# Where the head of each feed-forward layer puts its products, and which engine adds its weight blocks

## The chip, the cores and the metric

The kernel runs on one core of a Trainium2 chip. The metric is the device time in microseconds of one execution; of three executions of the kernel before, the median was 2402.97 us (2402.32 to 2407.87). The profile comes from one further execution, whose own time was 2399.43 us. Its records span 2397.6 us, and all times in rows are counted from the start of that span.

## The reference

One inference step of a streaming encoder with two layers, for 512 prompt tokens and 32 sample tokens, which the kernel handles together as 544 token columns. Each layer is a feed-forward block, a mixer (attention with a gated recurrence, or a gated delta rule) and a second feed-forward block. The change touches the four feed-forward blocks alone:

```python
def swiglu(h, w_in, w_out):
    gate, up = jnp.split(h @ w_in, 2, axis=-1)
    return (jax.nn.silu(gate) * up) @ w_out

x = x + 0.5 * swiglu(rms_norm(x, ffn1_norm[layer]), ffn1_w_in[layer], ffn1_w_out[layer])
```

The width of the model is 1024, the hidden width 2816. Everything is float32, and the result has to be nearly as exact as float32.

## The kernel before

**Three products for one.** Each float32 weight block and each activation is split into a high part (rounded, written by ScalarE, `op_split_hi`, L767) and a low part (the difference, written by VectorE, `op_split_lo`, L773). TensorE multiplies high by high, high by low and low by high and adds the three in PSUM.

**Units.** The hidden width is cut into 11 pairs of units of 256 columns. Unit `s = 0` of a pair is the gate, unit `s = 1` the value that the gate multiplies. Of one feed-forward layer the units are, in TensorE's order: unit 0 (kind "whole") and units 1, 2, 3 (kind "plain", 4 blocks of 24 matmuls each), which are the head. They give the first two pairs. Then come nine pairs in which each unit is of the kind "seven": the 2x2 block product of a unit is done with seven block products in place of eight (a Strassen-like scheme), at 12 matmuls each. It needs four sums and differences of weight blocks per unit, `wsum`, and seven token operands, `bop`, which are made once per layer in the head: sums in `bopf` (`token_sum`, L1054), then high parts (`bop_split_hi`, L926) and low parts (`bop_split_lo`, L932). After each of the pairs 2 to 9 a "mid" unit (4 blocks of 24 matmuls) multiplies part of the hidden activations by `w_out` and adds it to `x` (`x_update`, L1192). Four "last" units end the layer. So unit 4 is the gate and unit 5 the value of the first pair of the kind seven, and unit 6 is the first mid unit.

**What sets the order.** Nothing is scheduled by a planner: each engine runs a list of instructions written out by hand and waits on semaphores in that order. An instruction that waits holds back all that stands behind it on its engine. The splits of unit u+1 are made while TensorE works on unit u, in a ring of 8 blocks (`entry`), of which each is free again when TensorE has used it. Raw weights come in by a queue of SyncE into two buffers, `raw[0]` and `raw[1]`; a buffer is loaded again when all blocks of its unit are split.

**Copies that TensorE waits for.** In a seven unit ScalarE copies four PSUM banks to SBUF (`m1c`, `m5c`, `u2c`, `u3c`, L1134). TensorE's third block waits for the first copy, its fourth for the second, its fifth for the third, its seventh for the fourth (`ffn_seven_pe`). VectorE then adds the pieces (L1211, L1214, L1221).

**The hidden products of the head.** For pair j of the head VectorE multiplies the gate by the value out of PSUM (`hidden`, L1048), ScalarE makes the high part (`hidden_hi`, L911) and VectorE the low part (`hidden_lo`, L916). In the kernel before, those of the second pair close the head's lists on both engines. The sums of weights of units 4 and 5 are made by GpSimd (`weight_sums`, L1000 to L1005), those of the other 16 seven units of a layer by VectorE (`weight_sum_dve`, L1016 to L1024).

## Time and profile before

| What | Value |
|---|---|
| Median of 3 executions | 2402.97 us |
| The profiled execution's own time | 2399.43 us |
| Its span | 2397.6 us |
| TensorE busy | 2321.1 us, 97% |
| VectorE busy | 1656.8 us, 69% |
| ScalarE busy | 1061.9 us, 44% |
| GpSimd busy | 352.4 us, 15% |
| Mean granted TensorE clock | 0.990 |

TensorE is busy in nearly the whole span, so a stretch in which it has nothing to do is what there is to be looked for. In the rows PE is TensorE, DVE is VectorE, ACT is ScalarE, POOL is GpSimd. A line of the view in order of time gives start and duration in us, engine, line of the kernel, operation, what is written and read, the shapes and how many instructions are merged in it; in square brackets stands how long the engine sat idle before it, and what ended that.

### The profile page before, as it was taken

What the parts mean: (1) busy time and instruction counts of PE and PEld (TensorE: products, weight loads), DVE (VectorE), ACT (ScalarE), POOL (GpSimd) and SP (SyncE); (2) the same over time, 40 slices, a digit from 0 to 9 for tenths busy, and PEclk for the clock granted to TensorE, in tenths of its full rate; (3) what the DMA queues carried; (4) which work ended last, traced back from release to release, by engine and by line L of the source; (5) the groups of instructions that cost most, each with busy time, mean ns of one, the idle gap of its engine ahead of it and who ended that gap; (6) DMA issues with size and microseconds to landing.
All of it is one profiled execution on the core that took longest, in us unless ns stands there. A gap on an engine that the chain in (4) does not pass through costs nothing.

```text
span 2397.6 us, 44509 instructions
## 1 busy us (share of the span) xinstructions
PE 2321.1 (97%) x18296; PEld 2263.3 (94%) x18296; DVE 1656.8 (69%) x2657; ACT 1061.9 (44%) x1951; POOL 352.4 (15%) x284
## 2 busy tenths in 40 slices
PE   7899999999999899999899999999999999899998
PEld 7899999988989899999899999999999899899998
DVE  6867776656575877776866776788655657776674
ACT  3544444333323444444444444455345543444443
POOL 2300001000042300001400000243033533200001
PEclk9999999999999999999999999999999999999999
DMA  3223223322202232222232232322200012223222
GB/s 111 88 89 106 89 99 106 97 89 85 69 10 88 71 106 89 99 96 89 71 105 89 90 105 89 100 71 89 77 25 2 10 43 90 71 89 106 89 85 77
DMA packets 174905, 194.70 MB, mean 81 GB/s; under 512 B 4810, under 2 KB 155726, under 8 KB 174697
## 3 DMA queue, kind: packets, MB, share of 16 engines
q1 hardware_dynamic: 161902, 181.64, 23.0%
q10 hardware_dynamic: 12162, 8.11, 1.2%
q8 instruction: 147, 2.41, 0.4%
q0 software_dynamic: 640, 2.10, 0.3%
q14 instruction: 54, 0.44, 0.1%
HBM read 185.73 MB, written 6.10 MB: 80 GB/s over the span
## 4 chain that ended last, share of the span: by engine, by line
PE 88%; DVE 7%; issue 2%; ACT 1%; POOL 0%; DMA 0%; ACTq 0%; DVEq 0%
PE ps L852 32%; PE ps L782 25%; PE ps L659 19%; PE ps L3067 1%; DVE wl L773 1%; PE ps L3052 1%; DVE bop L932 1%; PE ps L3198 1%; DVE bopf L938 1%; DVE wl L644 1%; PE ps L3040 1%; PE ps L1637 0%; DVE bopf L1054 0%; PE ps L2105 0%; PE ps L2202 0%
## 5 line engine op out<-in xcount | busy, mean ns | idle before, releaser
L852 PE MATMUL ps<-bop,wh 128*128 128x272 f32 x4032 | 771.6, 291 | 36.2 <-ACT m1c L1134 33.0
L852 PEld LDWEIGHTS ps<-bop,wh 128*128 128x128 f32 x4032 | 639.5, 190 | 37.6 <-issue 33.8
L852 PE MATMUL ps<-bop,wl 128*128 128x272 f32 x2016 | 586.7, 291 | 0.0
L773 DVE TENSOR_TENSOR wl<-raw,wh 128x512 fp32r<-128x512 f32 (+1 forms) x456 | 318.0, 708 | 295.9 <-ACT wh L767 290.7
L852 PEld LDWEIGHTS ps<-bop,wl 128*128 128x128 f32 x2016 | 382.5, 190 | 0.0
L767 ACT ACTIVATE wh<-raw 128x512 fp32r<-128x512 f32 (+1 forms) x456 | 263.8, 609 | 222.4 <-PE ps L782 185.1
L782 PE MATMUL ps<-hh,wh 128*128 128x288 f32 (+1 forms) x1408 | 290.2, 287 | 0.0
L782 PE MATMUL ps<-hl,wh 128*128 128x288 f32 (+1 forms) x1408 | 289.6, 287 | 0.0
L782 PE MATMUL ps<-hh,wl 128*128 128x288 f32 (+1 forms) x1408 | 288.6, 286 | 0.0
L659 PE MATMUL ps<-xh,wh 128*128 128x288 f32 x1088 | 233.0, 295 | 3.4 <-DVE wl L644 2.8
L659 PE MATMUL ps<-xl,wh 128*128 128x288 f32 x1088 | 224.8, 288 | 0.0
L659 PE MATMUL ps<-xh,wl 128*128 128x288 f32 x1088 | 224.0, 287 | 0.0
L782 PEld LDWEIGHTS ps<-hh,wh 128*128 128x128 f32 x1408 | 215.0, 188 | 6.0 <-issue 6.0
L782 PEld LDWEIGHTS ps<-hh,wl 128*128 128x128 f32 x1408 | 215.2, 188 | 0.0
L782 PEld LDWEIGHTS ps<-hl,wh 128*128 128x128 f32 x1408 | 214.7, 188 | 0.0
L767 ACT ACTIVATE wh<-wsum 128x512 fp32r<-128x512 f32 x256 | 159.6, 627 | 109.4 <-DVE wsum L1016 83.4
L692 POOL COPY ssq<-sq 128x544 f32<-128x544 f32 x7 | 5.2, 743 | 1296.4 <-ACT sq L678 1296.4
L773 DVE TENSOR_TENSOR wl<-wsum,wh 128x512 fp32r<-128x512 f32 x256 | 175.2, 684 | 17.6 <-ACT wh L767 13.9
L659 PEld LDWEIGHTS ps<-xh,wh 128*128 128x128 f32 x1088 | 166.9, 189 | 15.4 <-issue 7.4
L659 PEld LDWEIGHTS ps<-xh,wl 128*128 128x128 f32 x1088 | 167.0, 189 | 0.0
L659 PEld LDWEIGHTS ps<-xl,wh 128*128 128x128 f32 x1088 | 166.7, 189 | 0.0
L644 DVE TENSOR_TENSOR wl<-raw,wh 128x2048 fp32r<-128x2048 f32 x41 | 94.5, 2305 | 39.7 <-ACT wh L639 39.7
(475 smaller groups left out, 3750.2 us busy)
## 6 DMA issues: line engine op xcount, KB each, us to landing
raw<-ffn_w_in SPq DMA_DIRECT2D x88, 1024.0 KB, 5.1
raw<-ffn_w_out SPq DMA_DIRECT2D x32, 1024.0 KB, 5.0
raw<-odd_w_in SPq DMA_DIRECT2D x16, 1024.0 KB, 5.7
raw<-even_w_in SPq DMA_DIRECT2D x14, 1024.0 KB, 5.1
raw<-ffn_w_out SPq DMA_DIRECT2D x16, 768.0 KB, 4.2
raw<-even_w_out SPq DMA_DIRECT2D x4, 1024.0 KB, 4.9
raw<-odd_w_out SPq DMA_DIRECT2D x4, 1024.0 KB, 5.2
xnat<-x_prompt SPq DMA_DIRECT2D x2, 1024.0 KB, 12.0
```

Source lines behind the costliest of these rows:

```text
L644: nc.vector.tensor_tensor(wl[slot][:, 0:kt, :], raw[slot][:, 0:kt, :], wh[slot][:, 0:kt, :].bitcast(F32), ALU.subtract).then_inc(lo_done.s ...
L659: ins = nc.tensor.matmul(ps[:, 2 * pe_out + b, PCOLS[b]], w, r[:, rk, TOKENS[b]], start=first and a == 0, stop=last and a == 2)
L767: nc.scalar.activation(entry(op)[0][:, 0:block_nk(u, i), :], op_source(u, i), ACT.Copy).then_inc(op_hi.sem, 1)
L773: nc.vector.tensor_tensor(lo[:, 0:nk, :], op_source(u, i), hi[:, 0:nk, :].bitcast(F32), ALU.subtract).then_inc(op_lo.sem, 1)
L782: ins = nc.tensor.matmul(ps[:, 2 * pe_out + b, PCOLS[b]], w[:, k, :], r[:, rk + k, TOKENS[b]], start=first and k == 0 and a == 0, stop=las ...
L852: ins = nc.tensor.matmul(ps[:, bank, 0:TH], w[:, k, :], bop[:, r, k, :], start=i in S_OPEN and k == 0 and a == 0, stop=k == KH - 1 and a = ...
L932: nc.vector.tensor_tensor(bop[:, o, :, :], bopf[:, o, :, :], bop[:, 7 + o, :, :].bitcast(F32), ALU.subtract).then_inc(bop_lo.sem, 1)
L938: nc.vector.scalar_tensor_tensor(out=bopf[:, first:first + 2, k % KH, :], in0=two(x[:, k, :]), scalar=gain(n, k), in1=two(rstd[:]), op0=AL ...
L3040: ins = nc.tensor.transpose(bank(g, 2, n, n)[:, h, :], dX[g][0:n, h, 0:n], ident[0:n, 0:n])
L3052: ins = nc.tensor.matmul(bank(g, 0, n, n)[:, h, :], strict[0:n, h, 0:n], dX[g][0:n, h, 0:n], start=True, stop=True)
L3067: ins = nc.tensor.matmul(bank(g, 0, n, n)[:, h, :], dU[g][0:n, h, 0:n], dZ[g][0:n, h, 0:n], start=True, stop=True)
L3198: ins = nc.tensor.matmul(ps[:, 2 * (2 * q + c) + b, PCOLS[b]], w, r[:, k, TOKENS[b]], start=k == 0 and a == 0, stop=k == KT - 1 and a == 2)
```

## The change

Two things are written in another way.

**The head's order.** The product of the second pair of the head, its high part and its low part leave the head's lists. The product (now `lead_product`) is issued by VectorE in unit 4, behind the fourth split of unit 5; its low parts and ScalarE's high parts are issued in unit 5. The low parts of the first pair go to unit 4. On ScalarE and VectorE the rest of the head is put in the order in which TensorE uses it: the token operands come earlier, and the weight sums of unit 4 are made by VectorE between them. The small `lam_dve` goes to the end of the head in the first layer.

**Who adds weight blocks.** Of a layer's 18 seven units GpSimd summed 2 (units 4 and 5) and VectorE 16. Now GpSimd sums the gate's unit of pairs 3 to 10, which is 8 units, and VectorE the other 10. GpSimd makes them as soon as the raw weights are there and the sums of the unit before are made. VectorE's list of each mid unit loses four sums by this.

```diff
@@ ffn_lead_act (ScalarE, head)
+        bop_split_hi(act, f, 0)
+        for i in range(4):
+            op_split_hi(act, units[3], i)
+        bop_split_hi(act, f, 1)
+        bop_split_hi(act, f, 2)
         hidden_hi(act, units[1], 0, 1)
         hidden_hi(act, units[1], 1, 2)
...
-        hidden_hi(act, units[3], 0, 1)
-        hidden_hi(act, units[3], 1, 2)
+        op_split_hi(act, units[4], 5)
+        op_split_hi(act, units[4], 6)
@@ ffn_lead_pool (GpSimd, head)
         gate(0, 0)
         gate(0, 1)
-        weight_sums(pool, ffns[f][4])
         gate(1, 0)
         gate(1, 1)
@@ weight_sum_dve
-        if s - first_seven[u.f] < 2:
+        if u.s == 0 and s != first_seven[u.f]:
             return
@@
+    def lead_product(dve, u, c):
+        dve.wait_ge(gate_rstd.sem, gate_rstd.at(2 * LEAD_PAIRS * u.f + 2 * u.pair + c + 1))
+        dve.wait_ge(op_used.sem, op_used.at(u.op + 2 * c + 2))
+        if u.pair:
+            dve.wait_ge(hl_ready.sem, hl_ready.at(2 * FJ * u.f + c + 1))
+        nc.vector.tensor_tensor(two(sq[c][:]), halves(2 + c), two(gbuf[c][:]), ALU.mult).then_inc(h_made.sem, 1)
+
+    def weight_sums_pool(pool, u):
+        s, slot, out = u.seven, u.raw % 2, sums_of(u)
+        pool.wait_ge(raw_loaded[slot].sem, raw_loaded[slot].at(8 * (u.raw - slot) + 16))
+        pool.wait_ge(sum_made.sem, sum_made.at(4 * s))
+        pool.wait_ge(op_lo.sem, op_lo.at(sevens[s - 2].op + 5))
...
     def ffn_pool(pool, f, n):
         ffn_lead_pool(pool, f, n)
         for u in ffns[f]:
-            if u.kind == "seven" and u.at > 2 * LEAD_PAIRS:
-                if u.seven - first_seven[f] < 2:
-                    weight_sums(pool, u)
+            if u.kind == "seven" and u.s == 0 and u.seven != first_seven[f]:
+                weight_sums_pool(pool, u)
@@ ffn_lead_dve (VectorE, head), gate of the second pair
                 dve.wait_ge(op_used.sem, op_used.at(units[2 * j].op + 2 * c + 2))
+                dve.wait_ge(h_made.sem, h_made.at(2 * FJ * f + c + 1))
...
-        hidden(1, 0)
...
-        hidden(1, 1)
-        hidden_lo(dve, units[3], 0, 1)
-        hidden_lo(dve, units[3], 1, 2)
@@ ffn_seven_act, behind the fourth split
         late_act(act, ffns[u.f][u.at - 1])
+        if u.at == 2 * LEAD_PAIRS + 1:
+            hidden_hi(act, ffns[u.f][u.at - 2], 0, 1)
+            hidden_hi(act, ffns[u.f][u.at - 2], 1, 2)
@@ ffn_seven_dve, behind the fourth split
+        if u.at == 2 * LEAD_PAIRS:
+            for c in range(2):
+                hidden_lo(dve, ffns[u.f][1], c, c + 1)
+            for c in range(2):
+                lead_product(dve, before, c)
+            dve.wait_ge(h_made.sem, h_made.at(2 * FJ * u.f + 2 * LEAD_PAIRS))
+        if u.at == 2 * LEAD_PAIRS + 1:
+            for c in range(2):
+                hidden_lo(dve, ffns[u.f][u.at - 2], c, c + 1)
+            dve.wait_ge(hl_ready.sem, hl_ready.at(2 * FJ * u.f + 2 * LEAD_PAIRS))
```

**VectorE from the end of the head into unit 4, first layer.** `wl` from `wsum_first_70` are splits of unit 4, from `wsum_first_71` of unit 5; L1048 is the product, L916 its low part. Before:

```order
L932 TENSOR_TENSOR bop<-bopf,bop 128x1088
L1048 TENSOR_TENSOR sq<-ps,gbuf_68 128x544
L773 TENSOR_TENSOR wl<-wsum_first_70,wh 128x512
L932 TENSOR_TENSOR bop<-bopf,bop 128x1088
L773 TENSOR_TENSOR wl<-wsum_first_70,wh 128x512
L773 TENSOR_TENSOR wl_50<-wsum_first_70,wh_49 128x512
L773 TENSOR_TENSOR wl_50<-raw,wh_49 128x512 x2
L1048 TENSOR_TENSOR sq<-ps,gbuf_69 128x544
L916 TENSOR_TENSOR hl<-sq,hh 128x544 x2
L773 TENSOR_TENSOR wl_50<-raw,wh_49 128x512
L773 TENSOR_TENSOR wl<-wsum_first_71,wh 128x512 x3
L1211 TENSOR_TENSOR gbuf_68<-u2c_78,ps 128x272
```

And now, from the first weight sum of unit 5 on (the product is L1016, the addition L1226):

```order
L1000 TENSOR_TENSOR wsum_first_71<-raw 128x512
L773 TENSOR_TENSOR wl_50<-raw,wh_49 128x512
L1003 TENSOR_TENSOR wsum_first_71<-wsum_first_71,raw 128x512
L773 TENSOR_TENSOR wl<-wsum_first_71,wh 128x512
L1006 TENSOR_TENSOR wsum_first_71<-raw,wsum_first_71 128x512
L773 TENSOR_TENSOR wl<-wsum_first_71,wh 128x512
L1008 TENSOR_TENSOR wsum_first_71<-raw 128x512
L773 TENSOR_TENSOR wl<-wsum_first_71,wh 128x512
L916 TENSOR_TENSOR hl<-sq,hh 128x544 x2
L1016 TENSOR_TENSOR sq<-ps,gbuf_68 128x544
L1016 TENSOR_TENSOR sq<-ps,gbuf_69 128x544
L1226 TENSOR_TENSOR gbuf_68<-u2c_78,ps 128x272
```

The products of the second pair stood among unit 4's splits and ahead of all of unit 5's; they now stand behind four splits of unit 5.

**ScalarE at the same place.** L911 is the high part of the hidden product, L1134 (now L1136) a copy that TensorE waits for. Before:

```order
L767 ACTIVATE wh_49<-wsum_first_70 128x512
L767 ACTIVATE wh_49<-raw 128x512 x2
L911 ACTIVATE hh<-sq 128x544 x2
L767 ACTIVATE wh_49<-raw 128x512
L1134 ACTIVATE m1c_74<-ps 128x272
L767 ACTIVATE wh<-wsum_first_71 128x512
```

And now:

```order
L767 ACTIVATE wh_49<-wsum_first_70 128x512
L926 ACTIVATE bop<-bopf 128x1088
L767 ACTIVATE wh_49<-raw 128x512 x3
L1136 ACTIVATE m1c_74<-ps 128x272
L767 ACTIVATE wh<-wsum_first_71 128x512
L1136 ACTIVATE m5c_76<-ps 128x272
```

The two high parts that stood ahead of the copy `m1c` are gone from here.

**VectorE at the start of a mid unit.** L1182 is the last product of the pair, `wsum_72` the sums of the next gate's unit, L1192 the first update of `x`. Before:

```order
L1182 TENSOR_TENSOR sq<-ps,gbuf_69 128x272
L1016 TENSOR_TENSOR wsum_72<-raw 128x512
L773 TENSOR_TENSOR wl<-raw,wh 128x512
L1019 TENSOR_TENSOR wsum_72<-wsum_72,raw 128x512
L773 TENSOR_TENSOR wl<-wsum_72,wh 128x512
L1022 TENSOR_TENSOR wsum_72<-raw,wsum_72 128x512
L1024 TENSOR_TENSOR wsum_72<-raw 128x512
L916 TENSOR_TENSOR hl<-sq,hh 128x544
L1192 SCALAR_TENSOR_TENSOR x<-ps,x 128x544
```

And now:

```order
L1187 TENSOR_TENSOR sq<-ps,gbuf_69 128x272
L773 TENSOR_TENSOR wl<-raw,wh 128x512
L773 TENSOR_TENSOR wl<-wsum_72,wh 128x512
L916 TENSOR_TENSOR hl<-sq,hh 128x544
L1197 SCALAR_TENSOR_TENSOR x<-ps,x 128x544
```

Four instructions between the last product and the first update have left VectorE's list; they are GpSimd's now.

## Rows read from the trace of the kernel before

**Rows 1.** The page, part 1: busy time, share of the span, instructions.

```profile
PE 2321.1 (97%) x18296; PEld 2263.3 (94%) x18296; DVE 1656.8 (69%) x2657; ACT 1061.9 (44%) x1951; POOL 352.4 (15%) x284
```

**Rows 2.** Waits of PE: us in total, times, longest us.

```profile
PE ps L852 <- ACT m1c L1134: 33.0, 4, 8.9
PE ps L852 <- DVE wl L773: 3.2, 3, 1.4
```

**Rows 3.** Timeline of PE: starts of units 4, 5 and 6, four layers.

```profile
80.96 0.41 PE L852 MATMUL ps<-bop,wh 128*128 128x272 f32 x2
...
92.75 0.79 PE L852 MATMUL ps<-bop,wh 128*128 128x272 f32 x2 [8.04 <-ACT m1c L1134]
...
101.63 0.42 PE L852 MATMUL ps<-bop,wh 128*128 128x272 f32 x2
...
112.23 0.42 PE L782 MATMUL ps<-hh,wh 128*128 128x288 f32 x2
...
804.97 0.41 PE L852 MATMUL ps<-bop,wh 128*128 128x272 f32 x2
...
827.61 0.42 PE L852 MATMUL ps<-bop,wh 128*128 128x272 f32 x2
...
1189.13 0.41 PE L852 MATMUL ps<-bop,wh 128*128 128x272 f32 x2
...
1210.51 0.42 PE L852 MATMUL ps<-bop,wh 128*128 128x272 f32 x2
...
2046.40 0.41 PE L852 MATMUL ps<-bop,wh 128*128 128x272 f32 x2
...
2069.48 0.42 PE L852 MATMUL ps<-bop,wh 128*128 128x272 f32 x2
```

**Rows 4.** Timeline of ACT, end of the first layer's head.

```profile
91.14 0.66 ACT L911 ACTIVATE hh<-sq 128x544 fp32r<-128x544 f32 x1 [4.63 <-DVE sq L1048]
91.71 0.61 ACT L767 ACTIVATE wh<-raw 128x512 fp32r<-128x512 f32 x1
92.23 0.38 ACT L1134 ACTIVATE m1c<-ps 128x272 f32<-128x272 f32 x1
```

**Rows 5.** Timeline of DVE, same place.

```profile
78.80 2.38 DVE L932 TENSOR_TENSOR bop<-bopf,bop 128x1088 fp32r<-128x1088 f32 x1
...
85.12 0.71 DVE L1048 TENSOR_TENSOR sq<-ps,gbuf 128x544 f32<-128x544 f32 x1
...
86.79 1.28 DVE L932 TENSOR_TENSOR bop<-bopf,bop 128x1088 fp32r<-128x1088 f32 x1
88.00 1.28 DVE L773 TENSOR_TENSOR wl<-wsum_first,wh 128x512 fp32r<-128x512 f32 x2
...
90.40 0.71 DVE L1048 TENSOR_TENSOR sq<-ps,gbuf 128x544 f32<-128x544 f32 x1
```

**Rows 6.** Timeline of POOL, same place: first and last sum of unit 5.

```profile
78.29 1.75 POOL L1000 TENSOR_TENSOR wsum_first<-raw 128x512 f32<-128x512 f32 x1
...
84.01 2.31 POOL L1005 TENSOR_TENSOR wsum_first<-raw 128x512 f32<-128x512 f32 x1
```

**Rows 7.** Timeline of DVE, second layer's head: products of the first pair.

```profile
785.14 1.34 DVE L1048 TENSOR_TENSOR sq<-ps,gbuf 128x544 f32<-128x544 f32 x2
```

**Rows 8.** The page, part 6: DMA issues, KB each, us to landing.

```profile
raw<-ffn_w_in SPq DMA_DIRECT2D x88, 1024.0 KB, 5.1
```

**Rows 9.** Timeline of DVE, second half of unit 5 and start of unit 6.

```profile
107.33 0.69 DVE L773 TENSOR_TENSOR wl<-raw,wh 128x512 fp32r<-128x512 f32 x1 [5.65 <-ACT wh L767]
...
109.00 0.69 DVE L773 TENSOR_TENSOR wl<-raw,wh 128x512 fp32r<-128x512 f32 x1 [0.60 <-ACT wh L767]
...
112.90 0.43 DVE L1182 TENSOR_TENSOR sq<-ps,gbuf 128x272 f32<-128x272 f32 x1
...
117.50 0.71 DVE L1192 SCALAR_TENSOR_TENSOR x<-ps,x 128x544 f32<-128x544 f32 x1
```

**Rows 10.** Timeline of PE, unit 6: its third block.

```profile
118.36 0.49 PE L782 MATMUL ps<-hh,wh 128*128 128x288 f32 x2
```

More of the change, by code:

```diff
@@ L1065, in ffn_lead_dve @@
             bop_normed(dve, f, n, k)
+        token_sum(3, 7, 6, 4, 0)
         op_split_lo(dve, units[2], 0)
-        token_sum(3, 7, 6, 4, 0)
         op_split_lo(dve, units[2], 1)
@@ L1071, in ffn_lead_dve @@
         op_split_lo(dve, units[2], 2)
+        op_split_lo(dve, units[2], 3)
+        token_sum(2, 5, 3, 8, 1)
         token_sum(1, 5, 7, 8, 0)
[L1073 to L1079 removed]
+        token_sum(0, 4, 2, 8, 2)
+        lead_product(dve, units[1], 0)
+        lead_product(dve, units[1], 1)
+        bop_split_lo(dve, f, 0)
         for i in range(4):
             op_split_lo(dve, units[3], i)
+        gate(1, 0)
+        weight_sum_dve(dve, units[4], 0)
+        bop_split_lo(dve, f, 1)
+        weight_sum_dve(dve, units[4], 1)
+        bop_split_lo(dve, f, 2)
+        op_split_lo(dve, units[4], 0)
+        weight_sum_dve(dve, units[4], 2)
+        gate(1, 1)
+        op_split_lo(dve, units[4], 1)
+        bop_split_lo(dve, f, 3)
+        weight_sum_dve(dve, units[4], 3)
+        op_split_lo(dve, units[4], 2)
+        bop_split_lo(dve, f, 4)
+        op_split_lo(dve, units[4], 3)
+        bop_split_lo(dve, f, 5)
+        op_split_lo(dve, units[4], 4)
+        bop_split_lo(dve, f, 6)
+        op_split_lo(dve, units[4], 5)
+        op_split_lo(dve, units[4], 6)
         if f == 0:
             lam_dve(dve)
[L1084 to L1099 removed]
     def next_split(eng, split, u, place):
```

61 lines of the change are left out of this document (13 added, 48 removed).

## The prediction

> **What bounds the kernel now.** I read the page's busy times first. TensorE is busy in 97% of the span [rows 1], so a gain has to come from the remaining idle time or from slow matmuls. The view of who waited for whom, cut to TensorE, shows the idle time: 33.0 us in four waits of up to 8.9 us for ScalarE's copy `m1c`, and 3.2 us for VectorE's splits `wl` [rows 2]. Four is the number of feed-forward layers. The timeline of TensorE shows the place: unit 4, the first of the kind seven [rows 3]. A unit of seven blocks normally takes 112.23 - 101.63 = 10.60 us, so a block takes 1.51. From the start of unit 4 to that of unit 5 it is 20.67, 22.64, 21.38 and 23.08 us in the four layers [rows 3], 87.8 together, where 42.4 would do. So the heads lose 45.4 us. 36.2 of these are the waits; the other 9.2 are matmuls after them that run slower (a pair takes 0.79 us right behind the wait, 0.41 otherwise [rows 3]), 2.3 us per head.
>
> Why the copy comes late stands in the timelines of ScalarE and VectorE. ScalarE could copy at 82.5, when the first block is done, but its list has a high part of the hidden product ahead; it sits 4.63 us for that and copies only at 92.23 [rows 4]. What it waits for is VectorE's product at 90.40, which stands behind all splits of unit 4 [rows 5]. And these are late because low parts of the token operands take 2.38 us while GpSimd sums weights, and 1.28 when it doesn't [rows 5, 6].
>
> **Part 1: the head.** The product and its high and low parts leave the place ahead of the copy, so that wait goes. What is late next is VectorE's own list. I lay it out in the second layer, where the head is shortest. VectorE finishes the products of the first pair at 786.5 [rows 7]. The list from there to the end of the head is seven low parts of operands at 1.21 (86.79 to 88.00), eleven splits and four sums at 0.60 each (two splits take 1.28 with the last one's tail), two gate products at 0.64 (a product's 0.71 less the tail that the next one covers) [rows 5]: 8.5 + 9.0 + 1.3 = 18.8. GpSimd's eight sums of the head are gone; its two gate multiplications of the second pair stay and hold VectorE up by 2.38 - 1.28 = 1.1 each. So the head's list ends at 786.5 + 18.8 + 2.2 = 807.5. Unit 4 starts at 804.97 [rows 3] and needs its last block's operands at 804.97 + 6 x 1.51 = 814.0, so no block of unit 4 waits for a split.
>
> Inside unit 4, two things are due. First, the copy `m5c` must be done before the fourth block, at 809.5; ScalarE's list has ahead of it a split of unit 5's first sum. That sum is done at 807.5 + 0.6, the split 0.6 later, the copy 0.4 later: 809.1, with 0.4 to spare. Second, the hidden products of the second pair must be there when unit 5 starts, at 815.6: three more sums and four splits (7 x 0.6) and two low parts and two products (4 x 0.64) end at 814.9, 0.7 to spare. Both margins are thin, but no wait is left by this count. Cost of part 1: -45.4 us. A bound on the other side: every us that VectorE is later beyond the 0.4 becomes a wait of TensorE, once per layer.
>
> **Part 2: the sums on GpSimd.** They are off TensorE's path if VectorE isn't pushed. One deadline is already missed a little: the third block of a mid unit needs VectorE's first update of `x`, which in unit 6 runs from 117.50 to 118.21 [rows 9]; TensorE starts the block at 118.36 [rows 10], about 0.18 later than it could. So whatever moves this update moves TensorE, in all 32 mid units.
>
> What GpSimd costs I take from the head. Its sum takes 1.75 us from 78.29 but had to wait for VectorE until 78.80, so it needs 1.24 alone. VectorE's instruction of 78.80 then waits for GpSimd's end at 80.04 and is done 1.14 later. They take turns. A VectorE instruction that has an input in PSUM isn't touched: 0.71 us inside GpSimd's last sum, and 0.71 without [rows 5, 6].
>
> Now a steady pair, in the clock of rows 9. The raw weights of the next gate are requested when unit 5's last split is done, near 101.7, and land 5.1 us later [rows 8], at 106.8. VectorE is idle until 107.33 [rows 9]. GpSimd's four sums then end at 108.15, 109.9, 111.6 and 113.1, and VectorE's instructions with two inputs in SBUF between them at 108.6 (first split), 110.3 (second), 111.8 (an addition), 113.5 (third split). Left before the last product are a product 0.35, an addition 0.35, a split 0.60 and a product 0.64, so it starts at 115.5 where it now starts at 112.90 [rows 9]: 2.6 later. From there to the update it is 4.60 now, of which the four sums moved away are 2.40; so the update starts at 115.47 + 2.20 = 117.67, 0.17 later than now. Waits of 0.60 and less that VectorE has in this stretch pay for part of it. The bounds for a mid unit: if the sums fell wholly into VectorE's idle time the 0.18 would be won back; if each of the four costs its full 1.1 and nothing is absorbed, it is 4.4 - 2.4 = 2.0 us lost. I take 0.17, the value of the layout. For the 28 mid units with a steady pair before them: +4.8 us.
>
> The first mid unit of each layer is worse. VectorE enters unit 4 late by 2.5 and has 4 sums, 7 splits, 2 low parts, 2 products and 3 additions in it, 10.3 us, and is done at 817.8, 2.2 after unit 5's start instead of at it. The raw weights land later by as much, at 109.0 in the clock of rows 9, when VectorE is no longer idle; and unit 5 has the two moved low parts besides. From 109.0 the list to the last product is 5.1 us alone, the four turns cost 4.4 less some 0.2 of waits, and 2.2 follow: the update starts at 120.5 and ends at 121.1, 2.9 later than now. Three layers at 2.9 and the first at 2.2, since there the head's list ends 1.7 behind unit 4's start: +11 us. Bounds: 0 (all absorbed), and 5 per layer.
>
> The two high parts that ScalarE now has in unit 5 take 1.2 us and push its fourth copy to about 110.5; the seventh block is due at 101.63 + 9.08 = 110.71, so I cost it at nothing.
>
> In the Trainium skill, page SBUF — State Buffer, section Who interferes with whom, the port that VectorE's second input and GpSimd share is an exclusive lock that an instruction keeps to its end. That is the mechanism of rival (e); the rows of the head agree with it in kind, but show 1.10 us lost and not GpSimd's whole instruction, and I go by the rows.
>
> **Sum.** -45.4 + 4.8 + 11 = -29.6 us. Against the profiled execution's own 2399.4 this is 2369.8. The median shown is 3.5 us above that execution; for the median I forecast 2402.97 - 29.6 = 2373 us.
>
> **Rivals.**
> (a) The mid units come free. GpSimd's sums meet VectorE's idle time and its PSUM instructions more than I laid out, the update is early everywhere: -45.4 - 32 x 0.18 = -51, or 2352. For it speaks the 5.65 us that VectorE idles before 107.33 [rows 9]; against it, that the weights land only at 106.8.
> (b) A wait stays in the heads. If VectorE comes into unit 4 one us later than I count, the fourth block or unit 5's first waits. That is about 1 us, and if the clock falls again 2.3 more: 4 x 3.4 = +14, or 2387. For it speak the thin margins.
> (c) Slower: the shared port is dear in every pair. The update of `x` is pushed by 2.0 us in 28 mid units and by 5 in four: -45.4 + 56 + 20 = +31, or 2434. It decides where a mid unit loses more than 45.4 / 32 = 1.4 us on average, that is where the pair's last product starts later than 116.7 in the clock of rows 9. For it speaks that GpSimd's sums took about 2.3 us each in places [rows 6]; against it, that VectorE's waits and its PSUM instructions lie between.
> (d) The change only trades waits: ScalarE is late for the copies by splits of unit 5 that wait for sums now on VectorE, and TensorE gets the same 8 us at another block. About 2400. Against it: the layout has these sums 0.4 us ahead of their need.
> (e) Each turn costs VectorE the whole 1.24 us that GpSimd needs, in place of the 1.10 of rows 5: four turns of 0.14 in 32 mid units are +18, or 2391. Against it: no instruction in rows 5 pays that much.
>
> **Chances.** The forecast 0.53, with a range of its own of 2363 to 2384 (0 to 1 us per head, first mid units between 0 and 5). (a) 0.15, (b) 0.17, (c) 0.06, (d) 0.05, (e) 0.04. A measurement of this kernel tells about 0.3%, 7.2 us, from no change. The forecast, (a), (b) and (e) are faster by more than that, and a fifth of (d): 0.90. Half of (d), and those of (c) in which the loss just balances, are the same: 0.04. Slower: 0.06. For 8 in 10 I leave out (c), (d) and the lower half of (a): 2351 to 2394.
>
> **What would show it.** Head right: no wait of TensorE for `m1c` in unit 4, 10.6 to 11 us from unit 4's start to unit 5's in all four layers, no slow pairs there, GpSimd without sums in the head. Head wrong: a wait of about 1 us at the fourth block or at unit 5's first. Port right: GpSimd's sums start about 5.2 us after unit 5's start at 1.3 to 1.8 us each, VectorE's splits there take up to 1.8, the last product starts 2.6 later against TensorE than now, and the third block of a mid unit is late by some 0.35 us; the first mid unit of a layer by about 3. What would make the whole wrong is a mid unit that loses more than 1.4 us, or a head that still waits.

## The result, and the profile after the change

| | Before | After |
|---|---|---|
| Median | 2402.64 us (2400.74 to 2407.87, 4 executions) | 2372.49 us (2370.07 to 2375.44, 4 executions) |
| Profiled execution, its own time | 2399.43 us | 2370.07 us |
| Its span | 2397.6 us | 2368.3 us |
| Mean granted TensorE clock | 0.990 | 0.997 |

The changed kernel is faster by 1.3%: 0.9872 of the time before, with a 95% interval of 0.985 to 0.9893. The forecast was 2373 us, and 2369.8 for the profiled execution.

The page's busy times after the change, which answer to [rows 1]:

```profile
PE 2311.4 (98%) x18296; PEld 2254.8 (95%) x18296; DVE 1677.0 (71%) x2561; ACT 1056.7 (45%) x1951; POOL 491.7 (21%) x380
```

VectorE has 96 instructions fewer than before and is busy 20.2 us longer. Its splits of raw weights take 867 ns on average where they took 708, and GpSimd's sums pay too (the four groups take 1.31, 1.63, 1.63 and 1.52 us for one sum, where the forecast counted 1.24 for one alone). From the page's costliest groups, in the order busy us, mean ns:

```profile
L773 DVE TENSOR_TENSOR wl<-raw,wh 128x512 fp32r<-128x512 f32 (+1 forms) x456 | 389.7, 867 | 261.3 <-ACT wh L767 258.5
...
L1024 POOL TENSOR_TENSOR wsum<-raw 128x512 f32<-128x512 f32 x32 | 41.8, 1307 | 864.4 <-DMA raw<-ffn_w_in 864.4
```

Who TensorE waited for (us in total, times, longest us), as in [rows 2]:

```profile
PE ps L782 <- DVE x L1197: 12.1, 13, 2.9
```

The 33.0 us for `m1c` and the 3.2 us for `wl` are gone. In their place stands the update of `x` in the mid units, with 12.1 us (9.8 of it in the four first mid units), and one wait of 1.5 us for `m5c`. Both can be seen in TensorE's timeline. The starts of units 4, 5 and 6 are those of [rows 3]; a row in brackets is a wait:

```profile
77.98 0.41 PE L852 MATMUL ps<-bop,wh 128*128 128x272 f32 x2
...
84.19 0.49 PE L852 MATMUL ps<-bop,wh 128*128 128x272 f32 x2 [1.51 <-ACT m5c L1136]
...
90.30 0.42 PE L852 MATMUL ps<-bop,wh 128*128 128x272 f32 x2
...
100.90 0.42 PE L782 MATMUL ps<-hh,wh 128*128 128x288 f32 x2
...
109.92 0.37 PE L782 MATMUL ps<-hh,wh 128*128 128x288 f32 x1 [2.90 <-DVE x L1197]
...
797.62 0.41 PE L852 MATMUL ps<-bop,wh 128*128 128x272 f32 x2
...
808.21 0.42 PE L852 MATMUL ps<-bop,wh 128*128 128x272 f32 x2
...
827.67 0.49 PE L782 MATMUL ps<-hh,wh 128*128 128x288 f32 x2 [2.31 <-DVE x L1197]
```

Unit 4 of the first layer takes 12.32 us (before 20.67), that of the second 10.59 (before 22.64); the third and fourth take 10.59 too. To compare kernels I use one measure from this timeline for all of them. The head's loss is unit 4 less 10.59 us. A mid unit's loss is its first four block lengths, start to start, less 4 x 2.97. The rest is what TensorE spends outside the stretches from unit 1 to the end of each feed-forward layer. All in us, summed over the four layers; "steady" are the 28 mid units behind the first of each layer:

| Kernel | Units 1 to 3 | Unit 4's loss | Unit 5's loss | First mid units | Steady mid units | Feed-forward layers | Rest |
|---|---|---|---|---|---|---|---|
| before | 145.0 | 45.4 | 0.0 | 1.1 | 7.7 | 1486.7 | 910.9 |
| after | 142.8 | 1.7 | 0.8 | 14.1 | 11.0 | 1457.8 | 910.5 |

So the 28.9 us that the feed-forward layers won are 43.7 in the heads and 2.2 in units 1 to 3, less 0.8 in unit 5, 13.0 in the first mid units and 3.3 in the steady ones.

**The copy `m1c` is no longer late.** ScalarE at unit 4 of the first layer, to be read beside [rows 4]:

```profile
79.69 0.40 ACT L1136 ACTIVATE m1c<-ps 128x272 f32<-128x272 f32 x1 [0.82 <-PE ps L852]
83.13 0.63 ACT L767 ACTIVATE wh<-wsum_first 128x512 fp32r<-128x512 f32 x1 [3.04 <-DVE wsum_first L1000]
83.66 0.38 ACT L1136 ACTIVATE m5c<-ps 128x272 f32<-128x272 f32 x1
```

`m1c` now waits for TensorE alone. `m5c` is queued behind the split of unit 5's first sum, and this sum comes late here. VectorE's list, which answers to [rows 5], has the end of the head, unit 5's first sum and the second pair's product; the first three rows are of the first layer, the last three of the second:

```profile
80.63 1.28 DVE L773 TENSOR_TENSOR wl<-raw,wh 128x512 fp32r<-128x512 f32 x2
...
82.41 0.69 DVE L1000 TENSOR_TENSOR wsum_first<-raw 128x512 f32<-128x512 f32 x1
...
88.49 1.35 DVE L1016 TENSOR_TENSOR sq<-ps,gbuf 128x544 f32<-128x544 f32 x2
...
798.52 1.28 DVE L773 TENSOR_TENSOR wl<-raw,wh 128x512 fp32r<-128x512 f32 x2
799.72 0.68 DVE L1000 TENSOR_TENSOR wsum_first<-raw 128x512 f32<-128x512 f32 x1
...
805.81 1.34 DVE L1016 TENSOR_TENSOR sq<-ps,gbuf 128x544 f32<-128x544 f32 x2
```

In the second layer the sum starts 2.1 us after unit 4, in the first 4.4 us. Why, stands in the granted clock from unit 1 to unit 4 of the first layer. From the view of windows (stretch, its length, busy us of PE, PEld, DVE, ACT, POOL, the clock, DMA share, GB/s), first the kernel before and then the one after:

```profile
42.96:80.96 38.00, 38.00 (x289) 38.00 (x289) 35.92 (x44) 16.84 (x23) 17.03 (x10) 0.94 0.18 57
```

```profile
42.19:77.98 35.79, 35.79 (x289) 35.79 (x289) 35.65 (x46) 20.34 (x28) 9.58 (x4) 1.00 0.19 60
```

A clock of 1.00 is the level of 2.4 GHz; a value below it is a mean over parts at 2.4 and at 1.2 GHz. TensorE did the same 289 matmuls without a gap in both, in 38.00 us at a clock of 0.94 and in 35.79 at 1.00. Counted from unit 1, this execution reached unit 4 2.2 us earlier. VectorE's list did not come earlier with it: in e3_update_early below, whose head is the same, TensorE reaches unit 4 at 79.48, 1.5 us later than here, and VectorE's sum starts at 82.33, where it starts at 82.41 here.

**GpSimd's sums.** A steady pair of the first layer, whose mid unit starts at 137.13. GpSimd, which answers to [rows 6]:

```profile
131.68 1.30 POOL L1024 TENSOR_TENSOR wsum<-raw 128x512 f32<-128x512 f32 x1 [27.21 <-DMA raw<-ffn_w_in]
133.06 1.63 POOL L1026 TENSOR_TENSOR wsum<-wsum,raw 128x512 f32<-128x512 f32 x1
134.76 1.62 POOL L1028 TENSOR_TENSOR wsum<-raw,wsum 128x512 f32<-128x512 f32 x1
136.34 1.49 POOL L1029 TENSOR_TENSOR wsum<-raw 128x512 f32<-128x512 f32 x1
```

VectorE in the same stretch, which answers to [rows 9], and at the end the last product of the pair and the mid unit's first update:

```profile
132.23 1.30 DVE L773 TENSOR_TENSOR wl<-raw,wh 128x512 fp32r<-128x512 f32 x1 [5.64 <-ACT wh L767]
133.45 0.43 DVE L1226 TENSOR_TENSOR sq<-u2c,ps 128x272 f32<-128x272 f32 x1
133.90 1.33 DVE L773 TENSOR_TENSOR wl<-raw,wh 128x512 fp32r<-128x512 f32 x1
135.15 1.53 DVE L1229 TENSOR_TENSOR sq<-u3c,m5c 128x272 f32<-128x272 f32 x1
136.60 1.78 DVE L773 TENSOR_TENSOR wl<-raw,wh 128x512 fp32r<-128x512 f32 x1
...
140.24 0.43 DVE L1187 TENSOR_TENSOR sq<-ps,gbuf 128x272 f32<-128x272 f32 x1
...
142.43 0.71 DVE L1197 SCALAR_TENSOR_TENSOR x<-ps,x 128x544 f32<-128x544 f32 x1
```

VectorE's splits end 0.55 us after one of GpSimd's sums (133.53 after 132.98, 135.23 after 134.69, 138.38 after 137.83), the addition of 135.15 0.30 after: VectorE waits for the end of GpSimd's instruction, then runs its own, and GpSimd's next sum waits in turn. The addition with one input in PSUM (133.45) takes its usual 0.43. The last product starts 3.11 us after the mid unit, before it was 0.67 [rows 9]; the update starts 5.30 after it, before it was 5.27. So four sums less in VectorE's list pay for what the turns took, almost to the last tenth.

### The profile page after: what moved, and what is told of

The parts are those of the page before. It is cut to its first block, busy times and chain, and to the rows that moved or that the text cites. A ratio compares the mean times of both kernels' runs of the same rounds, so it can differ in the third digit from the quotient of the medians.

```text
span 2368.3 us, 44549 instructions
## 1 busy us (share of the span) xinstructions
PE 2311.4 (98%) x18296; PEld 2254.8 (95%) x18296; DVE 1677.0 (71%) x2561; ACT 1056.7 (45%) x1951; POOL 491.7 (21%) x380
## 4 chain that ended last, share of the span: by engine, by line
PE 84%; DVE 10%; issue 3%; ACT 1%; POOL 0%; DMA 0%; ACTq 0%; DVEq 0%; POOLq 0%
PE ps L852 29%; PE ps L782 24%; PE ps L659 19%; DVE wl L773 2%; PE ps L3082 2%; PE ps L3067 1%; DVE sq L1229 1%; PE ps L3213 1%; DVE hl L916 1%; DVE wl L644 1%; PE ps L3055 1%; PE ps L1652 0%; DVE sq L1240 0%; DVE x L1197 0%; PE ps L2120 0%
## 5 line engine op out<-in xcount | busy, mean ns | idle before, releaser
L852 PE MATMUL ps<-bop,wh 128*128 128x272 f32 x4032 | 763.9, 289 | 1.5 <-ACT m5c L1136 1.5
L773 DVE TENSOR_TENSOR wl<-raw,wh 128x512 fp32r<-128x512 f32 (+1 forms) x456 | 389.7, 867 | 261.3 <-ACT wh L767 258.5
L782 PE MATMUL ps<-hh,wh 128*128 128x288 f32 (+1 forms) x1408 | 291.8, 289 | 13.6 <-DVE x L1197 12.1
L782 PEld LDWEIGHTS ps<-hh,wh 128*128 128x128 f32 x1408 | 216.3, 189 | 19.9 <-issue 19.4
L1024 POOL TENSOR_TENSOR wsum<-raw 128x512 f32<-128x512 f32 x32 | 41.8, 1307 | 864.4 <-DMA raw<-ffn_w_in 864.4
L767 ACT ACTIVATE wh<-wsum 128x512 fp32r<-128x512 f32 x256 | 152.8, 621 | 21.0 <-PE ps L852 21.0
```

The source lines that it names most:

```text
L767: nc.scalar.activation(entry(op)[0][:, 0:block_nk(u, i), :], op_source(u, i), ACT.Copy).then_inc(op_hi.sem, 1)
L773: nc.vector.tensor_tensor(lo[:, 0:nk, :], op_source(u, i), hi[:, 0:nk, :].bitcast(F32), ALU.subtract).then_inc(op_lo.sem, 1)
L782: ins = nc.tensor.matmul(ps[:, 2 * pe_out + b, PCOLS[b]], w[:, k, :], r[:, rk + k, TOKENS[b]], start=first and k == 0 and a == 0, stop=las ...
L852: ins = nc.tensor.matmul(ps[:, bank, 0:TH], w[:, k, :], bop[:, r, k, :], start=i in S_OPEN and k == 0 and a == 0, stop=k == KH - 1 and a = ...
L1024: nc.gpsimd.tensor_tensor(out[:, 0, :, :], block_raw(u, 1, 0), block_raw(u, 1, 1), ALU.add).then_inc(sum_made.sem, 1)
```

## The experiments

The same measures of all the kernels below, each from its own profile (us):

| Kernel | Median us | Unit 4's loss | Unit 5's loss | First mid units | Steady mid units | Feed-forward layers | Rest |
|---|---|---|---|---|---|---|---|
| e1_dve_sums | 2360.94 | 0.1 | 0.0 | 6.6 | 7.7 | 1446.4 | 913.7 |
| e2_pool_sums_alone | 2408.09 | 48.8 | 0.0 | 1.9 | 12.7 | 1494.7 | 911.6 |
| e3_update_early | 2357.66 | 0.1 | 1.0 | 9.2 | 0.7 | 1443.0 | 911.8 |
| e6_move_alone | 2380.55 | 19.5 | 0.0 | 6.6 | 7.8 | 1465.7 | 911.4 |
| e4_fifth_sum | 2405.51 | 1.7 | 0.7 | 18.8 | 35.3 | 1486.7 | 917.4 |
| e5_writes_only | 2352.77 | 0.2 | 0.0 | 0.1 | 0.6 | 1432.9 | 920.2 |
| e5_again | 2346.64 | 1.7 | 0.0 | 0.1 | 0.6 | 1432.9 | 912.0 |
| e7_hidden_early | 2366.35 | 0.0 | 0.0 | 5.8 | 10.6 | 1448.9 | 916.7 |
| e8_all_dve | 2347.95 | 0.0 | 0.0 | 0.1 | 0.6 | 1433.5 | 912.5 |
| e9_all_pool | 2351.87 | 0.0 | 0.0 | 4.2 | 1.2 | 1437.4 | 911.8 |

A stretch without any loss still shows 0.02 to 0.03 per mid unit by this measure, 0.6 to 1.0 for the 28 steady ones; the column is no better than 0.4 us.

### The head's order with VectorE's sums (e1_dve_sums)

The changed kernel, but VectorE keeps the sums of the gate's units.

```diff
 def weight_sum_dve
-        if u.s == 0 and s != first_seven[u.f]:
-            return
 def ffn_pool
-            if u.kind == "seven" and u.s == 0 and u.seven != first_seven[f]:
-                weight_sums_pool(pool, u)
```

> The changed head is kept; the sums of the gates' units of pairs 3 to 10 go back from GpSimd to VectorE, at their old places in the mid unit. Theory (part 2 only costs, by turns on the shared port): the third block of the 28 steady mid units is back at 3.13 us from up to 3.7, that of the first mid unit of a layer is at about 4.3 us instead of 5.4 to 6.0, and the whole is about 12 us shorter than the changed kernel: 2360 us. Rival (GpSimd's work is part of the gain): VectorE becomes late for TensorE in the mid units and the whole is 2376 us or more.

Measured: 2360.94 us (2359.88 to 2368.17), 0.9838 of before, interval 0.982 to 0.9855. So the half of the change that gives sums to GpSimd made the kernel about 11.5 us slower than it would have been; the feed-forward layers of the two profiles differ by 11.4. TensorE's waits for the update, to be held against the 12.1 us above:

```profile
PE ps L782 <- DVE x L1192: 5.5, 4, 1.4
```

Four waits are left, one in each first mid unit, though GpSimd sums nothing. This part of the first mid unit's loss comes from the head's half of the change: VectorE's work that was moved into units 4 and 5. It is 6.6 - 1.1 = 5.5 us. The other 14.1 - 6.6 = 7.5, and 11.0 - 7.7 = 3.3 in the steady mid units, are there only with GpSimd's sums. Of the 7.5 us, 4.5 are later updates (the first layer's starts 8.16 us behind the mid unit's start in the changed kernel, 6.63 here), and 3.0 are slow matmuls behind two of the longer waits, told of below.

### GpSimd's sums with the old head (e2_pool_sums_alone)

The kernel before, with the gate's sums from the second pair of the kind seven on given to GpSimd.

```diff
 def weight_sum_dve
-        if s - first_seven[u.f] < 2:
+        if s - first_seven[u.f] < 2 or u.s == 0:
             return
 def ffn_pool
                 if u.seven - first_seven[f] < 2:
                     weight_sums(pool, u)
+                elif u.s == 0:
+                    pool.wait_ge(sum_made.sem, sum_made.at(4 * u.seven))
+                    weight_sums(pool, u)
```

> The kernel before, with only the sums of the gates' units of pairs 3 to 10 given to GpSimd; the head as before. Theory: each mid unit gets 0.1 to 0.2 us longer and nothing else moves, so 2406 to 2408 us against 2402.6; the heads still lose their 45 us. Rival (these sums are a gain by themselves): below 2400 us.

Measured: 2408.09 us (2407.18 to 2412.55), 1.0027 of before, interval 1.0016 to 1.0038. Alone, this half costs 6 us and gains nothing:

```profile
PE ps L852 <- ACT m1c L1137: 32.1, 4, 8.0
...
PE ps L852 <- DVE wl L773: 6.7, 5, 2.2
PE ps L782 <- DVE x L1195: 4.2, 13, 0.8
```

The waits for `m1c` are as before, and the update of `x` has become a wait in 13 mid units. The heads lose 3.4 us more than before, with longer waits for `wl`; the expectation had nothing for this, and why it is so stays open. In the steady mid units the sums cost 12.7 - 7.7 = 5.0 us here and 3.3 with the new head. In the first mid units this kernel loses 1.9 where the changed one loses 14.1: there the sums are dear only if VectorE comes late into them.

### The update of `x` first (e3_update_early)

The changed kernel, with VectorE's first update of a mid unit one instruction earlier, ahead of a low part. (The two `weight_sum_dve` calls that it also passes do nothing in a mid unit of the changed kernel, since GpSimd makes these sums.)

```diff
 def ffn_mid_dve
         op_split_lo(dve, v, 1)
+        x_update(dve, u, 0)
         weight_sum_dve(dve, v, 2)
         weight_sum_dve(dve, v, 3)
         hidden_lo(dve, before, 0, 1)
-        x_update(dve, u, 0)
```

> The changed kernel, with the first update of x in a mid unit one instruction earlier on VectorE, ahead of the low part of the hidden product. Theory (the third block waits for this update and nothing else): the third block of a steady mid unit falls from 3.1 to 3.7 us to 2.97 or 3.0, that of the first mid unit by 0.6 us; 12 to 14 us shorter than the changed kernel, 2359 us. Rival (the block is late for a split or for ScalarE): no change, 2372 us.

Measured: 2357.66 us (2356.54 to 2358.67), 0.9819 of before, interval 0.9803 to 0.9835. One low part of 0.6 us moved behind the update takes the steady mid units' loss from 11.0 to 0.7. So it was this one deadline that the steady mid units missed, and by less than 0.6 us. In the first mid units four waits remain:

```profile
PE ps L782 <- DVE x L1197: 7.3, 4, 2.3
```

### Moving the product alone (e6_move_alone)

The kernel before, with the hidden product of the second pair, its high and its low parts where the change puts them. The rest of the head's lists is the old one, and GpSimd sums there.

```diff
 def ffn_lead_act
-        hidden_hi(act, units[3], 0, 1)
-        hidden_hi(act, units[3], 1, 2)
 def ffn_lead_dve
-        hidden(1, 0)
...
-        hidden(1, 1)
-        hidden_lo(dve, units[3], 0, 1)
-        hidden_lo(dve, units[3], 1, 2)
 def ffn_seven_dve, behind the fourth split (ffn_seven_act with the high parts alike)
+        if u.at == 2 * LEAD_PAIRS:
+            for c in range(2):
+                ...
+                nc.vector.tensor_tensor(two(sq[c][:]), halves(2 + c), two(gbuf[c][:]), ALU.mult)
+        if u.at == 2 * LEAD_PAIRS + 1:
+            for c in range(2):
+                hidden_lo(dve, ffns[u.f][u.at - 2], c, c + 1)
```

> The kernel before, with only the product of the head's second pair and its high and low parts moved to units 4 and 5; the rest of the head's lists and all sums as before. Theory: the 8 us wait for the copy goes, but GpSimd's sums still hold VectorE up in the head, so TensorE waits 2 to 3.5 us per head for splits of unit 4, and the first mid unit loses about 1 us: 2372 to 2380 us. Rival (the reordering of the head's splits is needed for most of the gain): above 2390 us.

Measured: 2380.55 us (2378.91 to 2382.89), 0.9914 of before, interval 0.9899 to 0.9928. This is 0.6 us above the range that was expected. The wait for `m1c` is gone by the move alone, but VectorE's splits are late for unit 4 eight times, and the heads lose 19.5 us, where four times 2 to 3.5 us was expected:

```profile
PE ps L852 <- DVE wl L773: 12.9, 8, 2.2
```

VectorE and GpSimd there, in the first layer:

```profile
80.86 1.76 DVE L773 TENSOR_TENSOR wl<-wsum_first,wh 128x512 fp32r<-128x512 f32 x1
82.55 2.37 DVE L932 TENSOR_TENSOR bop<-bopf,bop 128x1088 fp32r<-128x1088 f32 x1
```

```profile
78.04 1.75 POOL L998 TENSOR_TENSOR wsum_first<-raw 128x512 f32<-128x512 f32 x1
79.87 2.21 POOL L1000 TENSOR_TENSOR wsum_first<-wsum_first,raw 128x512 f32<-128x512 f32 x1
```

So of the 45.4 us the moved product is worth 45.4 - 19.5 = 25.9. The other 19.4 (19.5 to the 0.1 of e1_dve_sums) come from the new order of the operands and from taking GpSimd's sums out of the head, which this experiment does not part from each other. The first mid units lose 6.6 us here as in e1_dve_sums. So that loss comes with the moved product and its parts, not with the new order of the rest.

### A fifth instruction on GpSimd (e4_fifth_sum)

The changed kernel with one more addition behind the four sums, which nothing else waits for (its semaphore is left out of the lines below).

```diff
 def weight_sums_pool
+        two512 = rstd[:, 0:512].rearrange("p (k n) -> p k n", n=P)
+        nc.gpsimd.tensor_tensor(ssq[:, 0:512].rearrange("p (k n) -> p k n", n=P), two512, two512, ALU.add)
```

> The changed kernel, with a fifth addition of the same size on GpSimd behind each gate's four sums; it reads rstd and writes a scratch tile that nobody reads. Theory (each GpSimd instruction costs VectorE one turn of 1.1 us on the port, and the update of x moves by it): the third block of a mid unit takes about 4.3 us instead of 3.1 to 3.7, 32 times about 1.1 us: 2405 to 2408 us. Rival (what counts is when the sums are ready): nobody waits for the fifth, so 2372 us.

Measured: 2405.51 us (2399.55 to 2408.01), 1.0009 of before, interval 0.9999 to 1.0019: the whole gain is gone. GpSimd's instruction and the one of VectorE that pays for it, in a steady pair:

```profile
138.86 1.49 POOL L1034 TENSOR_TENSOR ssq<-rstd 128x512 f32<-128x512 f32 x1
```

```profile
139.37 1.28 DVE L1241 TENSOR_TENSOR sq<-sq,gbuf 128x272 f32<-128x272 f32 x1
```

This product of two SBUF inputs took 0.43 us at the same place without it, so VectorE is 0.85 later. TensorE now waits in all 32 mid units:

```profile
PE ps L784 <- DVE x L1204: 40.7, 32, 3.7
```

The feed-forward layers take 28.9 us more than in the changed kernel, 0.90 per mid unit. That the median is 33.0 higher is not all due to the port: the profiled execution lost 6.9 us in the rest, in code that no kernel here touches (below). The fastest executions of the two kernels, 2399.55 and 2370.07, are 29.5 us apart, as the layers say. The expected number was met, and a part of it for another reason.

### GpSimd writes only (e5_writes_only, e5_again)

The changed kernel, with the four sums replaced by writes of zeros of the same size. The sums of the gate's units are left out of the computation.

```diff
-        nc.gpsimd.tensor_tensor(out[:, 0, :, :], block_raw(u, 1, 0), block_raw(u, 1, 1), ALU.add)
+        nc.gpsimd.memset(out[:, 0, :, :], 0.0)
... (the other three sums alike)
```

> The changed kernel, with GpSimd's four sums replaced by four memsets of the same tiles, so it writes but doesn't read; the sums of these units are left out of the computation. Theory (the port is shared for reads of two SBUF inputs): VectorE's splits in that stretch take 0.69 us and not up to 1.8, the third block of all 32 mid units takes 2.97 us, 2347 us. Rival (the order on VectorE and the late weights make the loss, not the port): the first mid unit of a layer keeps 4.5 us or more, 2365 us.

Measured: 2352.77 us in two executions (2350.64 and 2354.9), 0.9794 of before, interval 0.9775 to 0.9814. No mid unit lost anything, but the time was 6 us over the theory's. The profile put these in the mixer of the second layer, between the third and the fourth feed-forward layer, with a wait for `s` that the changed kernel's profile does not have, and longer ones for `db` (1.5 us there):

```profile
PE ps L2583 <- DVE db L2569: 2.9, 2, 2.5
PE ps L2650 <- DVE s L2792: 2.8, 1, 2.8
```

That stretch took 494.7 us in place of 487.2. Whether the writes cause it or the single execution was open, so the kernel was run again.

> The kernel of e5_writes_only once more: GpSimd writes zeros in place of the sums of the gate's units, so the sums are left out of the computation. In its first profile all eight first and all steady mid units were free of waits, but the stretch between the third and fourth feed-forward layer, whose code nobody touched, took 494.7 us in place of 487.2. If that is a matter of the single execution, the median of more of them comes to 2348 to 2349; if it belongs to GpSimd's writes in this kernel, it stays at 2352 to 2353.

Measured: 2346.64 us (2346.34 to 2347.86, 5 executions), 0.9765 of before, interval 0.9752 to 0.9779. It is not the kernel: in this profile the stretch took 487.2. GpSimd's writes and VectorE's split in a steady pair, whose mid unit starts at 134.05, first GpSimd:

```profile
128.60 0.53 POOL L1024 MEMSET wsum<- 128x512 f32 x1 [28.41 <-DMA raw<-ffn_w_in]
129.18 0.53 POOL L1026 MEMSET wsum<- 128x512 f32 x1
```

```profile
129.15 0.69 DVE L773 TENSOR_TENSOR wl<-raw,wh 128x512 fp32r<-128x512 f32 x1 [5.64 <-ACT wh L767]
```

The first split runs while GpSimd writes and takes 0.69 us, where the same split took 1.30 beside GpSimd's sums. The third split takes 0.69 too, in place of 1.78; here GpSimd is done before it starts. At the first pair two low parts of 128x544 that start at 97.75 run over the writes from 98.01 on and take 1.36 us together, where they took 2.47 beside the sums. So a write does not hold VectorE up. This is the most direct evidence for the mechanism: same list, same waits, and the loss of all 32 mid units is gone when GpSimd reads nothing. The writes are also shorter than the sums (0.53 us to 1.30 and more), so fewer of VectorE's instructions meet them; what sums of that length would cost was not run. The Trainium skill, page SBUF — State Buffer, section Who interferes with whom, says that a VectorE instruction with two SBUF inputs contends with a GpSimd instruction that reads SBUF, and not with one that only writes; the splits of 0.69 us beside writes and of 1.30 beside sums agree.

### The hidden parts early in unit 5 (e7_hidden_early)

The changed kernel, with high and low parts of the second pair ahead of unit 5's first copy on ScalarE and ahead of the fourth split on VectorE.

```diff
 def ffn_seven_dve (ffn_seven_act with the high parts alike, ahead of copy(0, u.s, m1c))
+        if u.at == 2 * LEAD_PAIRS + 1:
+            for c in range(2):
+                hidden_lo(dve, ffns[u.f][u.at - 2], c, c + 1)
         next_split(dve, op_split_lo, u, 3)
...
-        if u.at == 2 * LEAD_PAIRS + 1:
-            for c in range(2):
-                hidden_lo(dve, ffns[u.f][u.at - 2], c, c + 1)
```

> The changed kernel, with the high parts and low parts of the head's second pair at the start of unit 5, where both engines idle, and not behind the fourth split. Theory (the first mid unit of a layer loses by two causes, these low parts and the weights that land 2 us later): its third block falls from 5.4 to 6.0 us to about 4.5, unit 5 is back at 10.59 us, 2365 us. Rival (only the late landing counts): the third block stays at 5.4 us or more, 2371 us.

Measured: 2366.35 us (2363.38 to 2367.54), 0.9849 of before, interval 0.9834 to 0.9864, near the expected 2365. What the edit mends is seen in the first mid unit of the changed kernel, which starts at 100.90. VectorE there:

```profile
97.69 2.47 DVE L916 TENSOR_TENSOR hl<-sq,hh 128x544 fp32r<-128x544 f32 x2 [1.00 <-ACT hh L911]
...
109.06 0.71 DVE L1197 SCALAR_TENSOR_TENSOR x<-ps,x 128x544 f32<-128x544 f32 x1
```

The two low parts meet GpSimd's sums late in unit 5 and take 2.47 us (3.44, 3.32 and 3.18 in the other layers), where two such parts take 1.35 in unit 4; the update starts 8.16 us after the mid unit, in a steady pair 5.30. With the parts ahead of the sums the first mid units' loss falls from 14.1 to 5.8 us; 3.0 of these 8.3 are the slow matmuls behind two waits, which this profile does not have. The median shows 6.1 us; the profiled execution gained 8.9 in the feed-forward layers and had 6.2 us more of rest than the changed kernel's, so the size is better taken from the layers.

### All mends together, with and without GpSimd (e8_all_dve, e9_all_pool)

Both have the early update, the early hidden parts, and the first sum of unit 5 in the head. In e8_all_dve VectorE makes all sums, in e9_all_pool GpSimd those of the gate's units.

```diff
 def ffn_lead_dve
+        weight_sum_dve(dve, units[5], 0)
         op_split_lo(dve, units[4], 5)
         op_split_lo(dve, units[4], 6)
 def ffn_seven_dve
-        weight_sum_dve(dve, v, 0)
+        if u.at != 2 * LEAD_PAIRS:
+            weight_sum_dve(dve, v, 0)
 and the edits of e3_update_early and e7_hidden_early; e8_all_dve also that of e1_dve_sums
```

> All four remedies: the changed head, the gates' sums on VectorE, the first update of x ahead of the last two sums and the low part, the high and low parts of the second pair at the start of unit 5, and the first sum of unit 5 two splits earlier in the head. Theory: no loss left in the heads or in the mid units (third block 2.97 us everywhere), 2347 us. Rival (VectorE's list, four sums longer, is late elsewhere): above 2357 us.

Measured: 2347.95 us (2347.78 to 2354.74), 0.9783 of before, interval 0.9764 to 0.9802. This beats both kernels, by 54 us the one before and by 24.5 the changed one. All 32 mid units, and units 4 and 5 of all layers, run without a wait. Its busy times:

```profile
PE 2305.8 (98%) x18296; PEld 2255.1 (96%) x18296; DVE 1646.3 (70%) x2689; ACT 1063.8 (45%) x1951; POOL 298.9 (13%) x252
```

VectorE has 128 instructions more than in the changed kernel and is busy 30.7 us less.

> The changed kernel with the three later mends (update of x first, hidden parts of the second pair early in unit 5, one sum of unit 5 in the head), but with GpSimd keeping the sums of the gate's units. Theory: GpSimd's sums cost TensorE only where VectorE has no idle time left, which by the traces of e3_update_early and e7_hidden_early is the first mid unit of a layer. There the third block was started 1.84 us late with the early update (2.4 in the first layer), and the early hidden parts took 1.0 off it in three layers. So about 0.85 us is left in each of four first mid units, steady mid units lose nothing, and the time is e8_all_dve plus 3.5 us: 2351 to 2352. Rival: the early hidden parts and the early update win the same time and do not add, so 1.8 us is left in each layer and the wait for m5c of the first layer stays: 2348 + 4 x 1.8 + 1.5 = 2357 or more.

Measured: 2351.87 us (2351.22 to 2354.32), 0.9787 of before, interval 0.9773 to 0.98. The mends add: the steady mid units lose 1.2 us, and the first mid units 4.2, against 3.4 expected. The wait for `m5c` is gone too, but that the sum moved into the head did it is not shown: in both profiles TensorE came to unit 4 late enough (38.2 us for units 1 to 3 of the first layer in e8_all_dve, 37.4 in this one) that the kernels without this mend lost 0.2 us there or nothing. TensorE's waits for the update:

```profile
PE ps L782 <- DVE x L1198: 2.5, 4, 0.7
```

In the best lists GpSimd's sums are thus no help. By the feed-forward layers of the two profiles they cost 3.9 us (1437.4 less 1433.5). The medians differ by as much, but they do not show it by themselves: as ratios to the kernel before, measured beside each, they are 0.9787 and 0.9783, and the intervals overlap. The four waits of the first mid units, in one profile and not in the other, do.

## Why the prediction was right

Its steps, in the order of its text:

**The wait for `m1c` goes with the product: right.** No such wait is left [rows 2], and e6_move_alone shows it for the move alone.

**No new wait in the heads: right in three layers, wrong in the first.** In the second layer VectorE's list was to end 2.5 us behind unit 4's start; it ended at 799.8, 2.2 behind. The margin for `m5c` was put at 0.4 us, and it held there: the copy is done 0.8 us before the fourth block. In the first layer the list was to end 1.7 us behind (a number given without its working), and the sum started 4.4 behind. The step that failed took TensorE's arrival from the profile before, where it ran at a clock of 0.94 up to unit 4; at 1.00 it came 2.2 us earlier. The other 0.5 is `lam_dve` (0.57 us from 81.84 to 82.41), which the count left out. Two executions of the same kernel show that this is the cause: in e5_writes_only units 1 to 3 of the first layer took 37.3 us and unit 4 10.75, in e5_again 35.8 and 12.31. Price: 1.7 us, more than paid by the 2.2 us that TensorE was faster. The whole term: 45.4 us forecast, 43.7 measured.

**Steady mid units: right, a little dear.** The last product was to be 2.6 us later and was 2.44; the update 0.17 later and was 0.03 in the pair shown. The cost was to be 4.8 us and was 3.3. The layout of the turns was met within 0.2 us, counted from the mid unit's start: sums of 1.3 to 1.6 us, splits of up to 1.78.

**First mid units: right in kind, made of other parts.** 11 us forecast, 13.0 measured. The layers lost 2.9, 4.0, 3.8 and 2.4 more than before, where 2.2 and three times 2.9 were forecast. In the first VectorE came late into unit 4 by more than in the others; in e7_hidden_early, where the first layer's sum starts 1.3 us behind unit 4 and not 4.4, the first layer loses the least of the four (0.95 us to 1.5 to 1.75). In the second and third it is the clock: the wait was the 2.31 us of the fourth layer, but the matmuls behind it ran slow for 3 us:

```profile
827.00:833.00 6.00, 5.33 (x30) 5.36 (x31) 4.87 (x9) 1.66 (x3) 0.00 (x0) 0.72 0.26 90
...
1204.00:1209.00 5.00, 4.09 (x21) 4.12 (x22) 4.44 (x8) 1.26 (x3) 0.00 (x0) 0.66 0.37 129
```

The prediction had counted such a fall only for rival (b). By e1_dve_sums 5.5 of the 13.0 have nothing to do with GpSimd, 4.5 are the turns and 3.0 the two falls of the clock. The prediction named both of the causes on VectorE's list ("VectorE enters unit 4 late", "unit 5 has the two moved low parts besides"), and its sum could not say which weighed more. The runs do not part them fully either: e7_hidden_early moves the parts away from GpSimd's sums and into idle time at once.

**ScalarE's two high parts at nothing: right.** Unit 5 lost 0.8 us in all, 0.4 of it in the second layer, but not by them: in e1_dve_sums ScalarE's list has them at the same place, and unit 5 loses nothing. What came late were VectorE's low parts, which met GpSimd's sums. In the second layer of the changed kernel, VectorE and then TensorE at the start of the mid unit:

```profile
815.60 3.44 DVE L916 TENSOR_TENSOR hl<-sq,hh 128x544 fp32r<-128x544 f32 x2 [1.01 <-ACT hh L911]
```

```profile
819.18 0.49 PE L782 MATMUL ps<-hh,wh 128*128 128x288 f32 x2 [0.21 <-DVE hl L916]
```

In e1_dve_sums the same two low parts take 1.36 us. The prediction had no term for this deadline.

**The sum.** -45.4 + 4.8 + 11 = -29.6 was forecast. Measured are -43.7 + 3.3 + 13.0 + 0.8 - 2.2 = -28.8 in the feed-forward layers, and 0.4 in the rest. Small misses of both signs cancelled, and that the forecast for the profiled execution, 2369.8, was met to 0.3 us is luck: four executions lay between 2370.07 and 2375.44. Two sums of the prediction are off, without a part in the forecast: rival (b) multiplies 3.4 us where its terms give 3.3, and the terms of its own range (0 to 4 us in the heads, 0 to 20 in place of 11 in the first mid units) give 2362 to 2386, not 2363 to 2384.

**The rivals.** (a) needed free mid units; by e5_again and e8_all_dve they would have been worth 2347 to 2348 us, so its mechanism was real and its condition not met. (b) happened in one layer of four, mostly because TensorE came earlier and not VectorE later, and without a fall of the clock. (c) and (e) fell: a turn costs VectorE 0.61 to 1.09 us beyond the instruction's own time in the pair shown. That (c) was near is what e4_fifth_sum shows: one turn more, and TensorE pays 0.90 us of it in each mid unit. (d) fell with the heads.

What the prediction did not see is that the two halves of the change had opposite signs: the head's order alone gives 2360.94 us, and GpSimd's sums take 11.5 us of it back. Its own terms said so, since the only positive ones came from part 2.

## What to carry to other kernels

Work that is moved to GpSimd to relieve VectorE costs VectorE a turn for each instruction with two SBUF inputs that it meets; here four turns weighed as much as the four sums that left, so the move gained nothing even where it fitted best. Where VectorE idles or reads PSUM all through GpSimd's sums it might pay; no run here has such a place. Before moving work off an engine, look for the one instruction on its list that TensorE waits for and put it earlier: putting the update ahead of one low part was worth some 15 us. And a margin of 0.4 us read from one profile is none, if TensorE's clock in that stretch was not full.
